# Scan levels: queries without zeros, and the level products head by head on row halves

## The chip, the core and the metric

One core of one Trainium2 chip runs the whole program. The metric is the device time of one execution in microseconds (us), the median of several runs. The engines named here are PE (TensorE: matrix products; its weight loads are listed apart, as PEld), DVE (VectorE), ACT (ScalarE), POOL (GpSimd) and SP (SyncE, which issues weight transfers). The program's buffers lie in SBUF; `ps` is PSUM, eight banks of 128 partitions by 512 fp32 values.

## The reference, cut to what matters

Two blocks of a network on 512 tokens of width 1024. The second block has two layers, and each of them has, among its token mixers, a gated linear recurrence (HGRN2) that runs forward and backward over the tokens:

```python
def _hgrn2_scan(q, k, v, logf):        # q, k, logf: 512 tokens x 6 heads x 64
    ...                                # bc = running sum of logf inside a chunk
    # o_t = sum over s <= t of  (q_t . k_s . exp(bc_t - bc_s)) v_s,  per head,
    # and a state that is carried from chunk to chunk

o_f = _hgrn2_scan(qr, heads(k_f), vr, heads(logf_f))
o_b = flip(_hgrn2_scan(flip(qr), flip(heads(k_b)), flip(vr), flip(heads(logf_b))))
o_r = o_f + o_b
```

The decay `exp(bc_t - bc_s)` is different for each of the 64 key channels of a head, so it has to be put into the queries and the keys before they are multiplied. It is everything in fp32.

## The kernel before

**Units.** The program treats the scan of one layer (it has two such scans, one at about 2058 to 2176 us of the profiled span, one at about 2862 to 2984 us) as six units: three blocks of 128 partitions, each with two heads of 64 key channels (head 0 in partitions 0 to 63, head 1 in 64 to 127), times two directions (d = 0 and 1; u = 2 b + d). Blocks are numbered `blk` over both scans.

**Pairs.** The 512 tokens are four tiles of 128. Products between different tiles, and the plain diagonal, are the pair products (L1246): 64 rows by 128 weight columns, 128 token columns, the two heads in turn on the two row halves of the array, each head into a bank of its own (`pair_bank`: banks 0 and 1 for even j - d, 2 and 3 for odd). ACT copies them out (L1910).

**Levels.** What is left inside a tile of 128 tokens is done in seven levels of halving, `LEVELS = [64, 32, 1, 2, 4, 8, 16]` (in this order; index li). On a level with half length m each block of 2m tokens has m queries and m keys on its two sides, decayed to the border between them. DVE writes the exponents of all seven levels of a unit into `WL` (L2619, L2620), ACT takes the exponential of all seven at once (L1887), DVE multiplies the key side by the keys (`weigh_levels`, L2642), POOL multiplies the query side by the queries (`queries`, L2962) and writes it into a buffer of its own, `level_queries(v)`, in spare columns of X and H (`resid` and `hbuf` in the profile). v counts the levels through both scans. Then PE multiplies: four products per level, one per tile t (L1264). The 128 weight columns are the tile's tokens with both heads' channels in the rows; the moving operand has 128 columns, of which the first 64 are the queries of head 0 with zeros in rows 64 to 127, the last 64 those of head 1 with zeros in rows 0 to 63. The zeros are written once per scan (L3001, L3002). One bank of 512 columns per level, in turn over banks 1, 2, 3, 0, 1, 2, 3 for li = 0 to 6.

**Taking.** ACT copies the levels li = 0 and 1 into the diagonal tiles of `AM` (L1928), in order and after all pairs of the unit; DVE merges li = 2 to 6 (`merge`, L2661, two predicated copies per level, one per head). `level_taken` counts both. A level's product waits for its query (`query_ready`), for the keys (`level_weighed`) and, from li = 4 on, for the bank: level v - 4 has been taken.

**Order of PE in a unit.** Pair products; a piece of the next layer stage's product that needs no scan result (`early`, L1311: ten 128x512 records per unit from the first levels on); for d = 0 and b >= 1 the sums of squares of the block before (`sum_rec`, L1330); the seven levels; for d = 0 the spread of its inverse root (`spread_rec`, L1339); for d = 1 the sum over the values (L1279), which waits until all 14 levels of the block have been taken. The first pair product of the next unit waits for all but the last two levels, those into banks 2 and 3 for all levels.

**Order of DVE in a unit.** `level_exponents(u+1)`, `weigh_ends(u+1)` (L2630, L2631), a finishing step of an earlier block (L2668, L2672, L2677), `merge(u)`, `weigh_levels(u+1)`. **ACT:** pair copies, a scaled copy for POOL (L1949), levels 0 and 1, `level_decays(u+1)` (L1887), a copy of sums, and the decays of the ends. **POOL:** `queries(u)`, an addition for the early piece (L2995), for every second unit the sum of the two directions' keys (L2983) and the power for the inverse root (L2973). POOL may run eight levels ahead of PE: `if v >= 8: pool.wait_ge(level_ready, v - 7)`.

All order is written out by hand, with semaphores; there is no planner.

Of the kernel before, what the change touches and what calls it, by code (L numbers as in the profile page):

```python
# [10 lines left out]
ALU = mybir.AluOpType  # L11
# [3 lines left out]
P = 128  # L15
D = 1024
KT = D // P
S = 512
C = 256
T = S + C  # L20
# [218 lines left out]
def build(nc, a, out):  # L239
    PHASES, CHUNKS = plan()  # L240
    with ExitStack() as ctx:
# [10 lines left out]
        X = sb("resid", [P, KT, T])  # L252
# [171 lines left out]
        def level_queries(v):  # L424

            k = v % 8
            return (X, H)[k // 4][:, 2 * (k % 4):2 * (k % 4) + 2, S:T]
# [486 lines left out]
        def level_bank(v):  # L914

            return (v % 7 + 1) % 4
# [64 lines left out]
        def _(pe):  # L981
# [234 lines left out]
            def scan(i):  # L1216
                n = scan_phases.index(i)
                for b in range(3):
                    blk = 3 * n + b
                    for d in range(2):  # L1220
# [5 lines left out]
                        for j in range(d, 4):  # L1226
                            if j == d and blk + d >= 1:

                                pe.wait_ge(level_taken, 14 * blk + 7 * d - 2)
# [22 lines left out]
                        for li in range(7):  # L1252
# [7 lines left out]
                            if li >= 4:  # L1260

                                pe.wait_ge(level_taken, v - 3)
                            for t in range(4):
                                mm = nc.tensor.matmul(ps[:, level_bank(v), t * P:(t + 1) * P], WL[:, 7 * (1 - d) + li, t * P:(t + 1) * P],  # L1264
                                                      level_queries(v)[:, t // 2, t % 2 * P:(t % 2 + 1) * P], start=True, stop=True)
# [223 lines left out]
        def _(act):  # L1489
# [359 lines left out]
            def scan(i):  # L1849
# [62 lines left out]
                def take_levels(u):  # L1912

                    blk, d = 3 * n + u // 2, u % 2
                    for li, m in enumerate(LEVELS[:PLAIN]):
# [7 lines left out]
                        for hx in range(2):  # L1923
                            for k in range(64 // m):
                                s0 = 2 * m * k + m * d
                                t0 = 2 * m * k + m * (1 - d)
                                from_ = ps[s0:s0 + m, level_bank(v), :].rearrange("p (t h x) -> p h t x", t=4, h=2)[:, hx, :, k * m:(k + 1) * m]
# [89 lines left out]
        def _(dve):  # L2017
# [577 lines left out]
            def scan(i):  # L2595
# [49 lines left out]
                def merge(blk, d):  # L2645

                    dve.wait_ge(pair_taken, pair_index(blk, d, 1, 3) + 1)
                    for li in range(PLAIN, 7):
# [9 lines left out]
                        for hx in range(2):  # L2658
                            dst = diagonal(hx).rearrange("p t (b x m) -> p t x b m", x=2, m=m)[:, :, 1 - d]
                            src = ps[:, level_bank(v), :].rearrange("p (t h b m) -> p h t b m", t=4, h=2, m=m)[:, hx]  # L2660
# [72 lines left out]
        def _(pool):  # L2733
# [173 lines left out]
            for i, ph in enumerate(PHASES):  # L2907
# [35 lines left out]
                elif kind == "scan":  # L2943
                    n = scan_phases.index(i)

                    def queries(u):
# [4 lines left out]
                        for li, m in enumerate(LEVELS):  # L2951
                            v = 42 * n + 7 * u + li
                            if v >= 8:

                                pool.wait_ge(level_ready, v - 7)
                            w = WL[:, 7 * (1 - d) + li, :].rearrange("p (t b x m) -> p t x b m", t=4, x=2, m=m)[:, :, 1 - d]
                            q = QR[:, b, :].rearrange("p (t b x m) -> p t x b m", t=4, x=2, m=m)[:, :, 1 - d]
                            dst = level_queries(v).rearrange("p a (c h b m) -> p a h c b m", c=2, h=2, m=m)
                            for hx in range(2):
                                rows = slice(64 * hx, 64 * hx + 64)  # L2960
                                for half in range(2):
                                    x = nc.gpsimd.tensor_tensor(dst[rows, half, hx], w[rows, 2 * half:2 * half + 2],  # L2962
                                                                q[rows, 2 * half:2 * half + 2], ALU.mult)
                            x.then_inc(query_ready, 1)
# [34 lines left out]
                    for half in (X, H):  # L2999
# [90 lines left out]
```

## Time and profile before

| | |
|---|---|
| median of 3 runs | 3423.84 us (3414.9 to 3428.85) |
| profiled execution | 3424.76 us |
| its span | 3422.7 us, so 2.06 us lie around the span |
| mean granted TensorE clock | 0.984 of full |
| PE busy | 3270.0 us |
| DVE, POOL, ACT busy | 2080.9, 1569.0, 968.0 us |

In the rows, PEclk is the granted clock of TensorE as a share of 2.4 GHz: 1.00 is the upper level, 0.50 the lower one (1.2 GHz). An fp32 product is two records, each with a weight load of its own: "x8" of L1264 is one level before the change. An idle time in brackets names what ended it.

### The profile page before, as it was taken

Reading aid. Unit: us, or ns where it says so; the run is one execution under the profiler, and the core shown is the slowest. Engines: PE = TensorE matmul, PEld = TensorE weight load, DVE = VectorE, ACT = ScalarE, POOL = GpSimd, SP = SyncE. Lnnn points to the kernel's source line nnn. Section 1 sums busy time; section 2 is a strip of 40 time slices with the busy share of each in tenths; the row PEclk is TensorE's granted clock in tenths of the full one; section 3 lists DMA queues with packets and bytes.
Section 4 is the critical chain, followed back from the end, with each engine's and each line's share of the span. In section 5 each row is a group of like instructions: output and inputs, shape, how many; then the busy total and the mean of one; then the engine's idle time right before and its main releaser. Section 6 shows DMA issues by size and latency. Waiting matters only on the chain. (4 is left out here: it accounts for less than half of the span.)

```text
span 3422.7 us, 44858 instructions
## 1 busy us (share of the span) xinstructions
PE 3270.0 (96%) x16138; PEld 2504.5 (73%) x16138; DVE 2080.9 (61%) x3509; ACT 968.0 (28%) x2213; POOL 1569.0 (46%) x1534
## 2 busy tenths in 40 slices
PE   7989999999999999999999978999999988999998
PEld 5666555555556967888888945688888865688887
DVE  7567756544444387455555668488764776656554
ACT  2066211001021165211122256322212236432211
POOL 1054323222235424544454548465645547755554
PEclk9999999999999999999999999999999998999999
DMA  7300223333312110344432200244443210022222
GB/s 251 125 23 2 99 86 123 117 117 105 123 57 65 66 38 14 105 158 165 157 124 85 85 20 14 77 149 156 156 150 102 88 46 16 20 92 87 87 87 80
DMA packets 91131, 317.88 MB, mean 93 GB/s; under 512 B 10817, under 2 KB 13153, under 8 KB 90913
## 3 DMA queue, kind: packets, MB, share of 16 engines
q1 hardware_dynamic: 64224, 218.34, 19.7%
q10 hardware_dynamic: 24768, 90.19, 7.2%
q0 software_dynamic: 1920, 6.49, 0.7%
q8 instruction: 132, 2.16, 0.3%
q14 instruction: 87, 0.70, 0.1%
HBM read 312.88 MB, written 2.10 MB: 92 GB/s over the span
## 5 line engine op out<-in xcount | busy, mean ns | idle before, releaser
L1354 PE MATMUL ps<-arena 128*128 128x256 f32 (+1 forms) x3744 | 952.4, 408 | 0.2
L1354 PEld LDWEIGHTS ps<-arena 128*128 128x128 f32 x3744 | 710.8, 190 | 205.0 <-issue 1.7
L2792 POOL TENSOR_TENSOR arena<-ring,arena 128x512 f32<-128x512 f32 (+1 forms) x140 | 181.6, 1297 | 837.0 <-PE ps L1354 837.0
L1354 PE MATMUL ps<-arena,ring 128*128 128x256 f32 (+1 forms) x2032 | 525.1, 410 | 3.1 <-ACT arena L1708 3.1
L1354 PE MATMUL ps<-hbuf,ring 128*128 128x256 f32 (+1 forms) x1824 | 471.6, 409 | 5.0 <-ACT hbuf L1815 2.0
L1354 PEld LDWEIGHTS ps<-arena,ring 128*128 128x128 f32 x2032 | 385.3, 190 | 119.8 <-ACT arena L1708 6.3
L1354 PEld LDWEIGHTS ps<-hbuf,ring 128*128 128x128 f32 x1824 | 349.0, 193 | 113.3 <-ACT hbuf L1815 16.2
L2330 DVE TENSOR_TENSOR arena<-ps,arena 128x256 f32<-128x256 f32 (+1 forms) x192 | 86.0, 448 | 357.0 <-PE ps L1354 235.9
L2217 DVE CUSTOM_DVE_ANT_0 aring<-aring,csil,adab 128x1024 f32<-128x1024 f32 x176 | 261.8, 1508 | 1.7
L2335 DVE SCALAR_TENSOR_TENSOR resid<-ps,mod,resid 128x256 f32<-128x256 f32 (+2 forms) x296 | 137.4, 482 | 185.4 <-PE ps L1354 180.3
L2775 POOL TENSOR_TENSOR arena<-ring 128x512 f32<-128x512 f32 (+1 forms) x140 | 181.2, 1294 | 141.3 <-PE ps L1354 133.2
L2335 DVE SCALAR_TENSOR_TENSOR resid<-arena,mod,resid 128x256 f32<-128x256 f32 (+1 forms) x168 | 109.2, 669 | 210.9 <-ACT arena L1708 207.6
L1708 ACT ACTIVATE arena<-ps 128x256 f32<-128x256 f32 (+1 forms) x152 | 62.9, 414 | 609.9 <-PE ps L1354 580.7
L2786 POOL TENSOR_TENSOR arena<-ring 128x512 f32<-128x512 f32 (+1 forms) x140 | 219.0, 1564 | 13.6 <-PE ps L1354 13.6
L1699 ACT ACTIVATE arena<-ps 128x256 f32<-128x256 f32 (+1 forms) x168 | 68.0, 405 | 476.0 <-PE ps L1354 465.7
L2781 POOL TENSOR_TENSOR arena<-arena,ring 128x512 f32<-128x512 f32 (+1 forms) x140 | 193.3, 1380 | 20.5 <-PE ps L1354 2.5
L2862 POOL TENSOR_SCALAR arena<-arena,small 128x512 f32<-128x512 f32 (+2 forms) x144 | 97.8, 691 | 209.1 <-DVE small L2098 209.1
L1354 PE MATMUL ps<-hbuf,arena 128*128 128x256 f32 (+1 forms) x672 | 175.8, 404 | 0.0
L2792 POOL TENSOR_TENSOR csil<-ring,junk 128x512 f32<-128x512 f32 x40 | 52.0, 1301 | 223.4 <-PE ps L1354 164.6
L1354 PEld LDWEIGHTS ps<-hbuf,arena 128*128 128x128 f32 x672 | 127.7, 190 | 34.4
L1672 ACT ACTIVATE rstd<-ps 128x256 f32<-128x256 f32 (+1 forms) x180 | 73.5, 408 | 253.6 <-PE ps L1354 236.3
L2424 DVE SCALAR_TENSOR_TENSOR arena<-arena 128x512 f32<-128x512 f32 x88 | 140.9, 1601 | 3.1
(327 smaller groups left out, 5209.3 us busy)
## 6 DMA issues: line engine op xcount, KB each, us to landing
aring<-in_ada ACTq DMA_DIRECT2D x172, 512.0 KB, 4.7
ring<-in_mlp SPq DMA_DIRECT2D x128, 512.0 KB, 3.8
ring<-in_up SPq DMA_DIRECT2D x88, 512.0 KB, 3.3
ring<-in_in SPq DMA_DIRECT2D x56, 512.0 KB, 3.3
ring<-in_down SPq DMA_DIRECT2D x32, 512.0 KB, 3.6
ring<-in_odd_in SPq DMA_DIRECT2D x24, 512.0 KB, 3.2
arena<-in_ada SPq DMA_DIRECT2D x16, 512.0 KB, 13.8
ring<-in_out SPq DMA_DIRECT2D x16, 512.0 KB, 3.2
```

The costliest lines, as they stand in the source:

```text
L1354: return nc.tensor.matmul(ps[:, bank, 0:p.tw], w, x, start=start, stop=stop, skip_group_check=True)
L1672: nc.scalar.activation(P1B[:, 0:tw], ps[:, XB[n % 2], 0:tw], ACT.Copy).then_inc(quick_act, 1)
L1699: nc.scalar.activation(second_sum(i, n)[:, 0:tw], ps[:, XB[n % 2], 0:tw], ACT.Copy).then_inc(quick_act, 1)
L2217: nc.vector.tensor_tensor_reduce(wt, wt, csil[:, 0, :], 1.0, adab[:, layer, nb:nb + 1], ALU.mult, ALU.add, mod[:, layer, nb, 0:1]).then_in ...
L2330: return nc.vector.tensor_tensor(home(p, half, lo, lo + tw), turned_view(p, product), turned_view(p, kept), ALU.add)
L2335: x = nc.vector.scalar_tensor_tensor(out=X[:, blk, a_:b_], in0=src[:, a_ - lo:b_ - lo], scalar=mod[:, layer, p.gate + blk, s_:s_ + 1], in1 ...
L2424: nc.vector.scalar_tensor_tensor(out=v, in0=u[:, 2:S + 2], scalar=CFW[:, blk, 2:3], in1=v, op0=ALU.mult, op1=ALU.add).then_inc(conv_out, 1)
L2775: nc.gpsimd.tensor_tensor(s[0], f1[:, 0:h], f1[:, h:2 * h], ALU.add).then_inc(wsum_ready, 1)
L2781: nc.gpsimd.tensor_tensor(s[1], s[0], f0[:, 0:h], ALU.subtract).then_inc(wsum_ready, 1)
L2786: nc.gpsimd.tensor_tensor(s[2], f0[:, 0:h], f1[:, 0:h], ALU.subtract).then_inc(wsum_ready, 1)
L2792: nc.gpsimd.tensor_tensor(s[3], f0[:, h:2 * h], s[1], ALU.subtract).then_inc(wsum_ready, 1)
L2862: nc.gpsimd.tensor_scalar(v, v, small[:, 12 + i % 4:13 + i % 4], 1.0, ALU.mult, ALU.mult).then_inc(pair_scaled, 1)
```

## The change

- POOL's queries of a level become one instruction of 128 partitions by 256 values (four tiles by 64), in place of four of 64 by 128. The buffer of a level is half as large, so there are 16 of them instead of 8, and POOL may run 16 levels ahead. The zeros and the four memsets per scan go.
- PE multiplies a level head by head, in turn on the row halves: eight products per level (16 records), each with 64 rows, 128 weight columns and 64 moving columns. Head 0 goes into one bank, head 1 into the next, 256 columns of each.
- So a level takes two banks. The pairs of banks are (2, 3), (0, 1), (2, 3), ... for li = 0, 1, 2, ...; from li = 2 on a level waits until level v - 2 has been taken (`v - 1` in the count). The first pair product of a unit waits for one level more than before.
- ACT and DVE read the same values from the new places, with as many instructions of the same sizes.

```diff
         def level_queries(v):
-            k = v % 8
-            return (X, H)[k // 4][:, 2 * (k % 4):2 * (k % 4) + 2, S:T]
+            k = v % 16
+            return (X, H)[k // 8][:, k % 8, S:T]
-        def level_bank(v):
-            return (v % 7 + 1) % 4
+        def level_bank(v, hx):
+            return 2 * ((v % 7 + 1) % 2) + hx
...
-                                pe.wait_ge(level_taken, 14 * blk + 7 * d - 2)
+                                pe.wait_ge(level_taken, 14 * blk + 7 * d - 1)
...
-                            if li >= 4:
-                                pe.wait_ge(level_taken, v - 3)
+                            if li >= 2:
+                                pe.wait_ge(level_taken, v - 1)
                             for t in range(4):
-                                mm = nc.tensor.matmul(ps[:, level_bank(v), t * P:(t + 1) * P], WL[:, 7 * (1 - d) + li, t * P:(t + 1) * P],
-                                                      level_queries(v)[:, t // 2, t % 2 * P:(t % 2 + 1) * P], start=True, stop=True)
+                                for hx in range(2):
+                                    rows = slice(64 * hx, 64 * hx + 64)
+                                    mm = nc.tensor.matmul(ps[:, level_bank(v, hx), 64 * t:64 * t + 64],
+                                                          WL[rows, 7 * (1 - d) + li, t * P:(t + 1) * P],
+                                                          level_queries(v)[rows, 64 * t:64 * t + 64], start=True, stop=True)
...
-                                from_ = ps[s0:s0 + m, level_bank(v), :].rearrange("p (t h x) -> p h t x", t=4, h=2)[:, hx, :, k * m:(k + 1) * m]
+                                from_ = ps[s0:s0 + m, level_bank(v, hx), 0:256].rearrange("p (t x) -> p t x", t=4)[:, :, k * m:(k + 1) * m]
...
-                            src = ps[:, level_bank(v), :].rearrange("p (t h b m) -> p h t b m", t=4, h=2, m=m)[:, hx]
+                            src = ps[:, level_bank(v, hx), 0:256].rearrange("p (t b m) -> p t b m", t=4, m=m)
...
-                            if v >= 8:
-                                pool.wait_ge(level_ready, v - 7)
+                            if v >= 16:
+                                pool.wait_ge(level_ready, v - 15)
...
-                            dst = level_queries(v).rearrange("p a (c h b m) -> p a h c b m", c=2, h=2, m=m)
-                            for hx in range(2):
-                                rows = slice(64 * hx, 64 * hx + 64)
-                                for half in range(2):
-                                    x = nc.gpsimd.tensor_tensor(dst[rows, half, hx], w[rows, 2 * half:2 * half + 2],
-                                                                q[rows, 2 * half:2 * half + 2], ALU.mult)
-                            x.then_inc(query_ready, 1)
+                            dst = level_queries(v).rearrange("p (t b m) -> p t b m", t=4, m=m)
+                            nc.gpsimd.tensor_tensor(dst, w, q, ALU.mult).then_inc(query_ready, 1)
...
-                    for half in (X, H):
-                        spare = half[:, :, S:T].rearrange("p k (c h v) -> p k h c v", c=2, h=2)
-                        nc.gpsimd.memset(spare[0:64, :, 1], 0.0)
-                        nc.gpsimd.memset(spare[64:P, :, 0], 0.0).then_inc(pool_step, 1)
-                        steps[0] += 1
-                        pool.wait_ge(pool_step, steps[0])
```

## Rows read from the trace of the kernel before

**Rows 1.** The page, part 1: busy time, share of the span, instructions.

```profile
PE 3270.0 (96%) x16138; PEld 2504.5 (73%) x16138; DVE 2080.9 (61%) x3509; ACT 968.0 (28%) x2213; POOL 1569.0 (46%) x1534
```

**Rows 2.** Line L1264: idle time before it, what ended it (us, times).

```profile
  POOL resid L2962: 14.8, 20
  POOL hbuf L2962: 14.1, 13
```

**Rows 3.** First scan by unit: busy us of PE, PEld, DVE, ACT, POOL; PEclk.

```profile
2057.89:2075.88 17.99, 13.97 (x98) 12.30 (x97) 11.76 (x29) 11.81 (x27) 15.98 (x32) 0.81 0.06 20
2095.96:2112.58 16.62, 15.77 (x133) 12.44 (x131) 12.06 (x28) 10.49 (x22) 15.60 (x28) 1.00 0.04 12
2112.58:2135.16 22.58, 18.55 (x107) 11.39 (x107) 22.00 (x48) 12.75 (x32) 21.22 (x39) 0.92 0.03 10
```

**Rows 4.** Groups by shape, POOL: busy us, mean ns, idle before.

```profile
L2962 POOL TENSOR_TENSOR resid<-arena 64x128 f32<-64x128 f32 x176 | 88.0, 519 | 8.5 <-issue 2.7
L2837 POOL TENSOR_TENSOR arena<-arena 128x256 f32<-128x256 f32 x24 | 15.9, 676 | 0.0
```

**Rows 5.** Timeline of PE, first scan: start us, us.

```profile
2051.30 6.66 PE L1311 MATMUL ps<-hbuf,ring 128*128 128x512 f32 x10 [4.71 <-ACT junk L1949]
...
2057.89 1.83 PE L1246 MATMUL ps<-arena 64*128 64x128 f32 x28
...
2062.30 3.80 PE L1264 MATMUL ps<-resid,arena 128*128 128x128 f32 x16 [0.82 <-POOL resid L2962]
2067.08 1.16 PE L1264 MATMUL ps<-resid,arena 128*128 128x128 f32 x8 [0.98 <-POOL resid L2962]
...
2103.93 0.95 PE L1330 MATMUL ps<-heads,arena 128*128 128x2 f32 x8
...
2129.88 5.35 PE L1279 MATMUL ps<-arena 128*64 128x512 f32 x16 [2.07 <-DVE arena L2661]
...
2138.74 4.56 PE L1311 MATMUL ps<-hbuf,ring 128*128 128x512 f32 x10
...
2143.94 3.82 PE L1264 MATMUL ps<-hbuf,arena 128*128 128x128 f32 x32
...
2166.95 3.65 PE L1279 MATMUL ps<-arena 128*64 128x512 f32 x16 [0.85 <-DVE arena L2661]
```

**Rows 6.** Timeline of DVE, first scan.

```profile
2056.81 2.44 DVE L2642 TENSOR_TENSOR arena<-arena 128x256 f32<-128x256 f32 x7 [7.25 <-ACT arena L1887]
...
2068.33 1.32 DVE L2661 COPY_PREDICATED arena<-arena,ps 128x256 f32<-128x256 int32 x2 [2.71 <-PE ps L1264]
...
2075.99 0.76 DVE L2661 COPY_PREDICATED arena<-arena,ps 128x256 f32<-128x256 int32 x2 [1.12 <-PE ps L1264]
2076.65 4.12 DVE L2642 TENSOR_TENSOR arena<-arena 128x256 f32<-128x256 f32 x7
...
2147.24 5.35 DVE L2661 COPY_PREDICATED arena<-arena,ps 128x256 f32<-128x256 int32 x10 [2.88 <-ACT arena L1928]
```

**Rows 7.** Timeline of ACT, unit 4 of the first scan.

```profile
2146.01 1.10 ACT L1928 ACTIVATE arena<-ps 32x128 f32<-32x128 f32 x4 [0.25 <-PE ps L1264]
```

**Rows 8.** Groups by shape, weight loads of the first scan: busy, mean ns.

```profile
L1246 PEld LDWEIGHTS ps<-arena 64*128 64x128 f32 x192 | 12.0, 187 | 9.2 <-ACT arena L1910 4.0 <-issue 2.4 <-DVE arena L2661 2.1
...
L1339 PEld LDWEIGHTS ps<-ident,small 128*64 128x64 f32 x43 | 2.3, 136 | 1.6 <-POOL small L2973 1.4
```

**Rows 9.** Chosen stretches: length, busy PE, PEld, DVE, ACT, POOL; PEclk.

```profile
1000.50:1004.00 3.50, 3.50 (x33) 3.50 (x33) 1.03 (x4) 0.94 (x2) 2.44 (x5) 1.00 0.34 81
1004.50:1007.50 3.00, 2.59 (x8) 2.01 (x9) 1.20 (x3) 0.06 (x1) 2.86 (x3) 0.50 0.21 71
...
2127.80:2130.60 2.80, 0.73 (x5) 0.34 (x6) 2.60 (x7) 2.15 (x8) 2.58 (x5) 1.00 0.02 6
2130.80:2134.00 3.20, 3.20 (x10) 0.96 (x8) 3.20 (x7) 0.00 (x0) 3.07 (x6) 0.50 0.00 0
```

**Rows 10.** Timeline of PE around 1001 us: what runs before the clock falls.

```profile
1001.44 2.82 PE L1167 MATMUL ps<-ones,arena 128*128 128x1 f32 x24
```

## The prediction

> **What bounds the kernel now.** I read the page first: TensorE is busy 96% of the span [rows 1], so what doesn't shorten or delay TensorE's own sequence changes nothing. Then I asked for the line of the level products. All its waits for POOL come to 14.8 + 14.1 = 28.9 us over both scans [rows 2], and PEld's waits are in that number together with PE's, so what PE itself lost is about half of it. That is a cap on what faster queries can give directly. Then the windows by unit and the timelines, to see where the waits lie. In unit 0 POOL sets the pace: it is busy 15.98 of 17.99 us, and the levels run from 2062.30 (first product) to 2076.65 (last merge done) [rows 3, 5, 6]. In unit 2 PE is busy 15.77 of 16.62 us, in unit 3 DVE 22.00 of 22.58 us [rows 3]: there POOL has caught up, four levels run without a gap in 3.82 us [rows 5], and the last wait before the values' product is for DVE's merge ([2.07 <-DVE], [0.85 <-DVE], rows 5). So the queries bound one unit in six; the others are bound by PE's order and by DVE's merges.
>
> **Queries.** A level's query is now four POOL instructions of 519 ns in the mean, 2.1 us; the nearest row for the new one is a 128x256 sum of POOL, 676 ns [rows 4]. Seven levels take some 5 us instead of 15. POOL drops out of the chain: in unit 0 the first product can start at about 2062.1 and never waits for a query again. The memsets lie before the scan in time that POOL spends waiting for ACT; I cost them at nothing.
>
> **Level product.** Before, a level is 8 records at 0.11 us, 0.9 us (3.82 for four, less the tail of the last). Is that the columns that stream, or the weights? The two-column products of L1330 tell: 8 records in 0.95 us, the same pitch as with 128 columns, so a 128-column weight load takes all of that pitch [rows 5]. The pair products, 64 rows in turn on two halves, run 28 records in 1.83 us, 0.06 us each: two halves at once, each again at 0.11 us [rows 5]. The new level has 16 records of that kind, so 16 x 0.06 = 0.9 us: no change, since the weights set the pace and only the streamed columns are halved. Loads of 64x128 take 187 ns in the record, those of 128x64 only 136 [rows 8]: the time goes with columns, not rows. The Trainium skill says the same (TensorE: Matmul & The Clock Gate, section "LDWEIGHTS (loading the stationary operand)": time is columns over 1.2 GHz, whatever the number of rows); the trace agrees. Bounds: 0.45 us if a half-height load with 64 columns took half, 0.9 us as taken. I take 0.9.
>
> **Two buffers in place of four.** A level is complete 1.16 us after its first record (the x8 row), DVE's merges take 1.32 us each for levels 2 and 3 and 0.76 for levels 4 to 6, with 0.1 between them 5.35 in all [rows 5, 6]. With P the start of the first level, ACT's copies of levels 0 and 1 end at P + 3.2 (2143.94 to 2147.11 in unit 4) and DVE starts merging at P + 3.3, 2147.24 [rows 5 to 7]. Now level 4 starts when level 2 is merged, D + 1.35 with D the start of merging, complete at D + 2.5, in time; level 5 starts when level 3 is merged, D + 2.8, complete D + 3.95, where DVE is ready at D + 3.65: 0.3 us late; level 6 follows at D + 3.7, complete D + 4.85. The merges end at D + 5.7 instead of D + 5.35, and DVE hears of the last level by a semaphore more: +0.4 us in each of 10 units (all but the two units 0), **+4 us**. Next in line, PE's values or pairs, waits for exactly this.
>
> **The clock.** This is the term that decides. Where the granted clock fell, PE had either stood idle much or streamed little. 1000.5 to 1004.0: PE and PEld busy for 3.50 of 3.50 us, but with one-column products (24 records of L1167); the next stretch is at 0.50 [rows 9, 10]. So weight loads by themselves don't hold it up. 2127.8 to 2130.6, the tail of a unit's levels and the wait for the merge: 0.73 us of PE, then 0.50, and the values' product took 5.35 us in place of 3.65 [rows 5, 9]. After the change a level streams half the columns in the same time, and from level 2 on its products come with gaps of 0.3 to 0.5 us. I expect the clock to fall in the second half of nearly every unit's levels, and to stay low until the values' product (odd units) or the early piece (even units) has run for a while. The prices, from rows at either level:
> - In unit 0 the clock is already low at the start: two levels took 3.80 us [rows 5]. Full-height products brought it back; half the columns won't. Seven levels at 1.75 us from 2062.1 end at 2074.4, the last merge at about 2075.3, against 2076.65. POOL's whole gain there is 1.4 us, in two scans **-3 us**.
> - In the other 10 units the last two levels run at 1.75 instead of 0.9: +1.7, less a little where DVE is late anyway: 1.6 x 10 = **+16 us**.
> - The values' product after levels: 5.35 instead of 3.65, for the 4 of 6 that now run at full clock, +1.7 each and +0.3 for the pairs that follow: **+8 us**.
> - After even units the spread, the pairs and the early piece: the ten-record piece took 6.66 us where it ran partly at the lower clock, against 4.56 [rows 5], +2.1 x 6 = 12.6. After units 0 and 2 DVE ends last anyway, by some 1.3 and 1 us, in two scans -4.6; one of these stretches is already low before the change, -1: **+7 us**.
>
> **DVE beside a lighter POOL.** The seven multiplications of `weigh_levels` take 2.44 us with POOL idle and 4.12 with POOL at work [rows 6]: the two disturb each other. POOL's bursts are now shorter but still begin shortly before these (they wait for the same ACT exponential), so I take half: 0.9 us, and it only counts where DVE ends last, twice per scan, and there mostly under the lower clock: **-1 us** (bounds 0 and -7). The Trainium skill has this as shared SBUF interfaces (GPSIMD Engine Reference, section "Key points"); the trace agrees with 2.44 against 4.12 us.
>
> **Sum.** -3 + 4 + 16 + 8 + 7 - 1 = +31 us on the profiled 3424.76 us, 3456 us. That execution lies 0.9 us over the median of the runs, so against 3423.84 it is +0.9%. I call within 0.5% (17 us) no change; the runs of before spread over 14 us.
>
> **Rivals.**
> 1. *The clock holds.* For it: PE and PEld stay as busy by the record, and the gaps are under half a microsecond each. Against it: the one-column row [rows 9, 10]. Then unit 0 runs its levels at about the present clock pattern and ends some 3.3 us (scan 1) and 4.6 us (scan 2) earlier, DVE's shorter multiplications give 1.3 x 2 + 0.4 x 2, the two buffers cost 4: -7.9 - 3.4 + 4 = -7, 3417 us. No change that can be told. It decides if the granted clock in units 1 to 5 stays above 0.95. Chance 0.19.
> 2. *Row halves really double the rate*: 0.45 us per level. Against it: L1330's pitch. It takes 0.7 us off the way to ACT's takes in the three units bound by PE, 0.7 x 6 = 4.2, and the 4 us of the two buffers vanish: -7 - 8 = -15, 3409 us with the clock held, the only way to come near -0.5%. The Trainium skill speaks for this one (TensorEngine Tiling (Array Packing), section "Theoretical Speedup": up to 2x for a small dimension of 64); by it this rival would be the result. Together with further savings on DVE over -0.5%: chance 0.03; otherwise with the clock fallen it only softens the forecast.
> 3. *The clock stays low through whole units*, from the levels over pairs and early piece into the next levels: then also the first levels (+1.7) and more of the pairs and the early piece (+2) run slow in the 10 units, +37 more, 3490 us. Chance 0.08.
>
> **How the numbers follow.** The forecast and its neighbours (the clock falls in most units, sum +17 to +55) have 0.70. Slower by over 0.5%: 0.70 + 0.08 - a tail of 0.04 where it falls but costs less than 17 us = 0.74; within 0.5%: 0.19 + 0.04 = 0.23; faster 0.03. The range reaches down to 3417 for rival 1 only in part: I set 3422 to 3488, which leaves about 0.16 below and 0.04 above; the forecast's own range is 3442 to 3475.
>
> **What would show it.** L2962 as 84 instructions of some 0.7 us and no PE wait for POOL in the scans (queries). L1264 with 16 records in 0.9 to 1.1 us where the clock is 1.00 (product). Merges of a unit in 5.7 us, PE waiting for DVE inside the levels (two buffers). PEclk by unit at 0.6 to 0.85 from unit 0 to 5, where it is 0.81 to 1.00 now [rows 3], and L1279 at over 5 us in most of six places (clock). What would make it wrong: a granted clock that doesn't fall at half the streamed columns; or falls that begin only after the unit's last level, so that the 16 us are not paid.

## The result, and the profile after

The changed kernel takes 3455.76 us (median of 4 runs, 3453.76 to 3459.49), the kernel before 3423.28 (4 runs beside it): ratio 1.0098, interval 1.0076 to 1.0121. It is slower by about 1%, and the forecast was 3456. The profiled execution took 3453.76 us (span 3451.9), 29.0 more than that of before; the medians lie 32.5 apart.

Part 1 of the page of the changed kernel, against [rows 1]:

```profile
PE 3311.1 (96%) x16810; PEld 2531.1 (73%) x16810; DVE 2074.7 (60%) x3509; ACT 968.3 (28%) x2213; POOL 1458.5 (42%) x1274
```

PE's busy time rose by 41 us although it streams fewer columns; POOL has 260 instructions fewer. POOL's queries by shape, after, against [rows 4]:

```profile
L2962 POOL TENSOR_TENSOR resid<-arena 128x256 f32<-128x256 f32 x44 | 34.7, 821 | 15.0 <-issue 9.5 <-ACT arena L1890 5.5
L2962 POOL TENSOR_TENSOR hbuf<-arena 128x256 f32<-128x256 f32 x40 | 31.3, 814 | 15.2 <-issue 12.5 <-ACT arena L1890 2.5
```

84 instructions, 66.0 us in all; a level's query costs 0.82 us where it cost 2.1. The waits of PE alone for its level products in the first scan, after (us, times, longest); [rows 2] has both scans and the weight loads too:

```profile
PE ps L1266 <- DVE arena L2664: 4.2, 12, 0.7
...
PE ps L1266 <- ACT arena L1931: 1.2, 5, 0.2
...
PE ps L1266 <- POOL resid L2962: 0.2, 1, 0.2
```

So the change did what it says: PE waits for POOL once, for 0.2 us, where it had waited eight times, 6.9 us, in this scan. It now waits for DVE, twelve times, inside the levels. The timeline of PE in the first scan, after (start us, us; in brackets the idle time before and who ended it), against [rows 5] (the lines have moved: L1266 is a level, L1282 the values' product, L1342 the spread, L1314 the early piece):

```profile
2062.13 3.04 PE L1266 MATMUL ps<-resid,arena 64*128 64x64 f32 x48 [0.63 <-ACT arena L1913]
...
2080.06 1.11 PE L1266 MATMUL ps<-resid,arena 64*128 64x64 f32 x16
2081.00 2.12 PE L1266 MATMUL ps<-hbuf,arena 64*128 64x64 f32 x32
2083.36 1.11 PE L1266 MATMUL ps<-hbuf,arena 64*128 64x64 f32 x16 [0.24 <-ACT arena L1931]
2084.82 1.11 PE L1266 MATMUL ps<-hbuf,arena 64*128 64x64 f32 x16 [0.34 <-DVE arena L2664]
2086.24 3.61 PE L1266 MATMUL ps<-hbuf,arena 64*128 64x64 f32 x32 [0.31 <-DVE arena L2664]
2090.71 6.55 PE L1282 MATMUL ps<-arena 128*64 128x512 f32 x16 [0.86 <-DVE arena L2664]
...
2112.21 2.40 PE L1266 MATMUL ps<-resid,arena 64*128 64x64 f32 x32 [0.31 <-DVE arena L2664]
2114.54 1.97 PE L1342 MATMUL ps<-ident,small 128*64 128x128 f32 x16
2116.44 2.98 PE L1246 MATMUL ps<-arena 64*128 64x128 f32 x24
2119.35 5.10 PE L1314 MATMUL ps<-hbuf,ring 128*128 128x512 f32 x10
```

Three levels (48 records) take 3.04 us, one level 1.11 with its tail: about 1 us, as before. A unit's last two levels take 3.61 us in unit 1 and 2.40 in unit 2 (2.0 at the upper clock), then the values' product 6.55 instead of 3.65, or the spread 1.97 instead of 1.09. Windows of the changed kernel (length, busy us of PE, PEld, DVE, ACT, POOL, then PEclk, the granted clock): the six units of the first scan (units 1, 3 and 5 without their values' product), and behind them four stretches, from the fourth level of unit 1 to the first pair products of unit 2.

```profile
2057.91:2072.64 14.73, 11.98 (x157) 10.76 (x156) 12.72 (x32) 12.15 (x29) 11.61 (x14) 0.89 0.08 24
2072.64:2090.71 18.07, 16.31 (x143) 12.56 (x143) 15.15 (x34) 10.60 (x24) 8.29 (x10) 0.78 0.06 19
2097.19:2114.54 17.35, 15.85 (x172) 12.44 (x171) 7.53 (x16) 11.17 (x24) 4.93 (x5) 0.97 0.05 13
2114.54:2134.95 20.41, 18.67 (x164) 14.59 (x163) 16.32 (x37) 12.18 (x31) 10.28 (x13) 0.75 0.03 11
2141.50:2158.78 17.28, 15.78 (x172) 12.38 (x171) 7.50 (x16) 9.91 (x20) 4.85 (x5) 0.98 0.05 13
2158.78:2176.62 17.84, 16.09 (x163) 12.20 (x163) 10.35 (x20) 4.39 (x13) 4.96 (x6) 0.88 0.04 12
...
2083.40:2086.20 2.80, 2.18 (x32) 1.93 (x32) 2.59 (x5) 2.80 (x1) 0.64 (x1) 1.00 0.03 6
2086.40:2090.00 3.60, 3.45 (x32) 3.26 (x31) 1.44 (x5) 3.40 (x12) 3.43 (x5) 0.50 0.00 0
2090.80:2096.80 6.00, 6.00 (x16) 1.63 (x16) 6.00 (x17) 0.00 (x0) 1.03 (x2) 0.52 0.00 0
2097.19:2100.70 3.51, 2.90 (x42) 2.46 (x40) 3.19 (x7) 2.82 (x7) 0.00 (x0) 1.00 0.02 5
```

The clock falls after the fifth level, with PE busy 2.18 of 2.80 us on half the columns; it stays at 0.50 while two levels keep PE busy for 3.45 of 3.60 us, and at 0.52 through 6.00 us of the values' product; behind that it is at 1.00. In the second scan the levels of unit 0, the pairs behind them and half of the early piece ran at 0.50, 17.00 us in one stretch (2881.7 to 2898.7), with PE busy for 16.68 of them. In the records of PE one can add up where the time of both scans went, from the first start of each stage to the first start of the next:

| stage, both scans (us) | before | after | after, 128 columns (e1_wide) | before, two buffers (e5_lock) |
|---|---|---|---|---|
| levels of unit 0 | 27.0 | 20.7 | 19.4 | 27.0 |
| levels of units 2 and 4 | 25.8 | 34.9 | 32.8 | 32.5 |
| levels of units 1, 3, 5 | 55.6 | 61.5 | 62.3 | 62.6 |
| values' product (6) | 25.5 | 37.5 | 21.5 | 21.5 |
| spread, rest of the pairs, early piece after even units | 49.0 | 55.2 | 43.9 | 42.7 |
| all else | 57.6 | 57.7 | 57.7 | 57.4 |
| sum | 240.5 | 267.5 | 237.7 | 243.8 |

27.0 of the 29.0 us lie in the two scans. The other 2 can't be told from chance: what lies outside the scans is the same program in all twelve profiles, and takes 3177 to 3188 us in them. The last two columns are experiments, below.

### The profile page after: what moved, and what is told of

It reads as the page before. It is cut to its first block and busy times, and to the rows that moved or that the text cites. A ratio compares the mean times of both kernels' runs of the same rounds, so it can differ in the third digit from the quotient of the medians.

```text
span 3451.9 us, 45966 instructions
## 1 busy us (share of the span) xinstructions
PE 3311.1 (96%) x16810; PEld 2531.1 (73%) x16810; DVE 2074.7 (60%) x3509; ACT 968.3 (28%) x2213; POOL 1458.5 (42%) x1274
## 5 line engine op out<-in xcount | busy, mean ns | idle before, releaser
L2789 POOL TENSOR_TENSOR arena<-ring 128x512 f32<-128x512 f32 (+1 forms) x140 | 218.9, 1563 | 11.9 <-PE ps L1357 11.9
L2784 POOL TENSOR_TENSOR arena<-arena,ring 128x512 f32<-128x512 f32 (+1 forms) x140 | 193.4, 1382 | 20.4 <-PE ps L1357 2.3
## 6 DMA issues: line engine op xcount, KB each, us to landing
arena<-in_ada SPq DMA_DIRECT2D x16, 512.0 KB, 13.7
```

Source lines behind the costliest of these rows:

```text
L2784: nc.gpsimd.tensor_tensor(s[1], s[0], f0[:, 0:h], ALU.subtract).then_inc(wsum_ready, 1)
L2789: nc.gpsimd.tensor_tensor(s[2], f0[:, 0:h], f1[:, 0:h], ALU.subtract).then_inc(wsum_ready, 1)
```

## The experiments

The time of the two scans in the profiled execution is given beside the whole time, since the scans are 7% of it and a few us of them vanish in the spread of the runs. Each scan time comes from one profiled execution, so a difference of one or two us between two of them isn't shown. The ratios are to runs of the kernel before on the same chip: median 3423.66 us for e1, e3, e4 and e5, 3425.97 for e6, e7, e9 and e10, 3426.14 for e11 and e12.

**e1_wide: the changed kernel with its 64 moving columns streamed twice.** The number of columns differs from the changed kernel, and with it the place of the results in their banks, from which ACT and DVE read as many values as before (that part is not shown).

```diff
-mm = nc.tensor.matmul(ps[:, level_bank(v, hx), 64 * t:64 * t + 64],
+mm = nc.tensor.matmul(ps[:, level_bank(v, hx), t * P:(t + 1) * P],
                       WL[rows, 7 * (1 - d) + li, t * P:(t + 1) * P],
-                      level_queries(v)[rows, 64 * t:64 * t + 64], start=True, stop=True)
+                      level_queries(v)[rows, 64 * t:64 * t + 64].unsqueeze(1).broadcast_to([64, 2, 64]), start=True, stop=True)
...
```

> The changed kernel, but each level product streams its 64 query columns twice, so 128 columns per weight load, and each head's products fill a whole bank; nothing else differs (queries, waits, two bank pairs, order), and all values that are used are the same. Clock theory: the weight loads set the pace, so a level still takes 0.9 us at the upper level, but the streamed columns keep the clock up: no fall inside the levels, the values' product back from 5.9 to 6.6 us to 3.65 in most of its six places, the two scans (240.5 us before, 267.5 after the change, from the first pair product to the first product behind them) take 230 to 236 us, the whole about 3416 us. Rival, two buffers or row halves: if the gaps for DVE or the alternation on halves cost the time, the scans stay at 260 us or more, the whole at 3450. Rival, product paced by columns: a level takes longer than 0.9 us.

Measured: 3420.9 us (12 runs; ratio to before 0.9989, interval 0.9980 to 0.9999), scans 237.7. Timeline of PE and windows (units 1 and 2) of e1_wide:

```profile
2079.56 1.16 PE L1266 MATMUL ps<-hbuf,arena 64*128 64x128 f32 x16 [1.27 <-DVE arena L2665]
2080.97 2.06 PE L1266 MATMUL ps<-hbuf,arena 64*128 64x128 f32 x32 [0.25 <-DVE arena L2665]
2083.89 3.65 PE L1283 MATMUL ps<-arena 128*64 128x512 f32 x16 [0.86 <-DVE arena L2665]
```

```profile
2072.60:2087.50 14.90, 12.33 (x133) 8.03 (x131) 13.99 (x28) 8.97 (x19) 8.33 (x9) 1.00 0.07 23
2087.50:2104.50 17.00, 15.65 (x172) 12.06 (x170) 10.85 (x26) 10.79 (x22) 4.55 (x5) 1.00 0.05 13
```

The same products with twice the columns take the same time each (1.16 against 1.11 us a level), the clock stays at 1.00 in these units, and the scans take 29.8 us less than in the changed kernel. That is the whole slowdown: with everything else of the change in place, it comes with the streamed columns, and the granted clock goes with it. What is left is a gain of 2.8 us and not the 7 I had for a clock that holds; 237.7 is above the 230 to 236 that I expected, 3420.9 above 3416.

**e5_lock: the kernel before, where PE waits for a level to be taken as if there were two level buffers.** Its four banks stay, and so does the first pair product's wait.

```diff
-                            if li >= 4:
+                            if li >= 2:
...
-                                pe.wait_ge(level_taken, v - 3)
+                                pe.wait_ge(level_taken, v - 1)
```

> The kernel before with only the wait of two buffers (from the third level on a level waits until the level two before it has been taken); it still has four banks. Two buffers by my sum: +0.4 us in 10 units, +4 us, scans 244 to 246 us, the whole 3427 us, as long as the clock stays as it is; products stream 128 columns, so short gaps should not bring it down much. If waiting itself made most of the loss, +20 us or more.

Measured: 3428.37 us (10 runs; 1.0013, 1.0003 to 1.0024), scans 243.8: 3.2 us more than before, where the forecast had 4. Its column of the table shows that this is a difference of large terms. The levels of ten units take 13.7 us longer, since PE is held back; of that 6.3 come back after the even units, where PE no longer has to wait behind the spread, and 4.0 in the values' product. PE and windows of e5_lock around unit 3, against [rows 5, 9]:

```profile
2128.90 1.13 PE L1264 MATMUL ps<-resid,arena 128*128 128x128 f32 x8 [1.74 <-DVE arena L2661]
2130.32 3.65 PE L1264 MATMUL ps<-resid,arena 128*128 128x128 f32 x16 [0.29 <-DVE arena L2661]
2134.82 3.65 PE L1279 MATMUL ps<-arena 128*64 128x512 f32 x16 [0.85 <-DVE arena L2661]
```

```profile
2130.00:2134.70 4.70, 3.68 (x17) 3.47 (x16) 2.40 (x8) 2.47 (x9) 4.35 (x8) 0.64 0.01 3
2134.90:2138.40 3.50, 3.50 (x16) 0.98 (x16) 3.50 (x7) 0.00 (x0) 3.37 (x6) 1.00 0.00 0
```

Before, the wait of 2.07 us came behind the last level. The clock was still at 1.00 until 2130.60, 0.7 us into the values' product, and at 0.50 from 2130.80 on, and this product paid (5.35 us) [rows 5, 9]. With the two-buffer wait the gap lies ahead of the last levels; the clock falls there too (two levels take 3.65 us), but it is back at 1.00 when the values' product starts, which runs in 3.65.

**e3_pool: the kernel before with the queries of the changed one**, products on all 128 rows with four banks. The zeros are left out, so its products mix the two heads; the buffers' places, POOL's wait and the memsets, which change as in the changed kernel, are not shown.

```diff
...
-                                                      level_queries(v)[:, t // 2, t % 2 * P:(t % 2 + 1) * P], start=True, stop=True)
+                                                      level_queries(v)[:, t % 2 * P:(t % 2 + 1) * P], start=True, stop=True)
...
-                            for hx in range(2):
-                                rows = slice(64 * hx, 64 * hx + 64)
-                                for half in range(2):
-                                    x = nc.gpsimd.tensor_tensor(dst[rows, half, hx], ...)
+                            nc.gpsimd.tensor_tensor(dst, w, q, ALU.mult).then_inc(query_ready, 1)
...
```

> The kernel before with POOL's part of the change alone: one instruction of 128x256 per level, 16 buffers, no memsets; PE multiplies as before, 128 rows and 128 columns, four bank buffers. Its products mix the two heads, since the zeros are gone: that is left out of the computation. All theories: this is what faster queries are worth with neither row halves, nor two buffers, nor fewer columns. By my terms the scans gain 7.9 us in the units 0 and about 3 us by DVE beside a lighter POOL: 229 to 233 us for both scans instead of 240.5, the whole about 3413 us. If POOL's gain had been there and been eaten by the rest of the change, it shows here; if POOL was never worth anything, 3423.

Measured: 3423.12 us (12 runs; 0.9997, 0.9988 to 1.0006), scans 242.6, 2.1 more than before and 10 over the most that I expected (233). The levels of unit 0 do take 17.7 us instead of 27.0. PE and windows of e3_pool at the end of unit 1:

```profile
2087.81 1.13 PE L1264 MATMUL ps<-hbuf,arena 128*128 128x128 f32 x8 [0.39 <-DVE arena L2661]
2091.74 5.23 PE L1279 MATMUL ps<-arena 128*64 128x512 f32 x16 [2.80 <-DVE arena L2661]
```

```profile
2088.95:2091.70 2.75, 0.00 (x0) 0.00 (x0) 2.44 (x8) 2.63 (x10) 2.75 (x5) 0.97 0.00 0
2091.80:2095.00 3.20, 3.20 (x8) 0.94 (x10) 3.20 (x6) 0.00 (x0) 1.99 (x3) 0.51 0.02 5
```

PE is done early, stands idle for 2.8 us until DVE has merged, and the values' product then runs at 0.51 for its first 3.2 us. It takes 5.2 to 5.4 us in all six places, 31.6 us in sum against 25.5. Of the 9.3 us that unit 0's levels gain, nothing is left: PE idles instead, and the clock is low behind the gap.

**e12_pool_lock: e3_pool with the wait of e5_lock.** It mixes the heads as e3_pool does.

```diff
-                            if li >= 4:
+                            if li >= 2:
...
-                                pe.wait_ge(level_taken, v - 3)
+                                pe.wait_ge(level_taken, v - 1)
```

> The kernel before with the fast queries and the wait of two buffers, 128 columns and full rows (its products mix the two heads, since the zeros are gone: that is left out of the computation). Against the variant with 64 columns streamed twice (237.7 us for both scans) only the row halves differ. If row halves cost nothing: 236 to 239 us. If each turn between half-height and full-height products costs some 0.1 to 0.2 us, as the spread pieces suggest (1.05 us from one to the next with halves, 0.87 without), 2 to 5 us less: 233 to 236. It also tells why fast queries alone gave nothing: if the values' product is back at 3.65 us here, the wait of two buffers kept the clock that they lost.

Measured: 3422.36 us (10 runs; 0.9992, 0.9982 to 1.0001), scans 236.6, the values' product at 3.65 us in all six units. So the two scans are 6 us shorter than in e3_pool with a wait more; the whole times (0.9992 and 0.9997) don't tell the two apart. The fast queries are worth 7.2 us where the wait stands (243.8 - 236.6). To e1_wide it is +1.1 (237.7 - 236.6): row halves, with their pairs of banks and the first pair product's longer wait. That lies in the range that I gave for row halves that cost nothing, and it is 3.0 us more in the units 0 and 1.9 less elsewhere, so no cost is shown by it.

**e4_cols and e7_cols_lock: the kernel before with 64 moving columns, with four buffers and with the two-buffer wait.** The rows stay whole, POOL stays slow. Head 1's products are left out, and ACT and DVE read head 0's for both (not shown); e7_cols_lock has the wait of e5_lock besides.

```diff
-mm = nc.tensor.matmul(ps[:, level_bank(v), t * P:(t + 1) * P], WL[:, 7 * (1 - d) + li, t * P:(t + 1) * P],
-                      level_queries(v)[:, t // 2, t % 2 * P:(t % 2 + 1) * P], start=True, stop=True)
+mm = nc.tensor.matmul(ps[:, level_bank(v), t * P:t * P + 64], WL[:, 7 * (1 - d) + li, t * P:(t + 1) * P],
+                      level_queries(v)[:, t // 2, t % 2 * P:t % 2 * P + 64], start=True, stop=True)
...
```

> The kernel before, but a level product streams only the first 64 of its 128 columns (head 0; head 1's level values are left out, both heads take head 0's). Full rows, four buffers, POOL as before with four instructions. Clock theory: the same weight loads, half the streamed columns, so the clock falls in the levels as in the changed kernel, although there are no row halves and no two buffers: PEclk of the scans 0.75 to 0.88, scans 250 to 262 us instead of 240.5, the whole 3433 to 3445 us. Rival, row halves or the two buffers: no change from 240.5 us and 3423.

> The kernel before with the 64 columns (head 0 alone; head 1's level values are left out) and the wait of two buffers, full rows, POOL as before. Alone the columns gave 252.4 us for both scans and the wait 243.7. Clock theory: the two together space thinly streaming products, the clock falls inside the levels and they wait for each other at the lower clock: 264 to 272 us, the same as the changed kernel with four POOL instructions, so that row halves cost nothing. If they only add (+11.9 + 3.2), 255.6 us, and then row halves would be the rest, 12 us or more.

Measured: e4_cols 3439.54 us (5 runs; 1.0043, 1.0027 to 1.0059), scans 252.4: +11.9, in the range, with PEclk 0.85 over each scan. So thin columns lower the clock with whole rows and four buffers too. e7_cols_lock 3451.99 us (4 runs; 1.0080, 1.0060 to 1.0099), scans 272.8, just over the 272 that I gave at most: +32.3 on before, and +29.1 on e5_lock, close to what the columns cost on row halves (29.8). So the wait costs 3.2 us with full columns and 20.4 with half (272.8 - 252.4), and the columns cost 11.9 without the wait and 29.1 with it: of the 32.3 us, 17.2 come only where the two stand together.

The granted clock sorts the twelve kernels by their columns alone. Over a whole scan it is 0.77 to 0.85 in the five that stream 64 columns, with whole rows (e4, e7) and on row halves (the changed kernel, e6, e11), and 0.93 to 0.99 in the seven that stream 128.

**e6_four_pool: the changed kernel with each query in four POOL instructions.**

```diff
-                            nc.gpsimd.tensor_tensor(dst, w, q, ALU.mult).then_inc(query_ready, 1)
+                            for hx in range(2):
+                                rows = slice(64 * hx, 64 * hx + 64)
+                                for half in range(2):
+                                    x = nc.gpsimd.tensor_tensor(dst[rows, 2 * half:2 * half + 2], ...)
+                            x.then_inc(query_ready, 1)
```

> The changed kernel with its queries written by four POOL instructions of 64x128 per level again; PE, the two buffers and the 64 columns stay. If the fast queries had kept some of their gain under the fallen clock (3 us by the prediction's unit 0), this is 3 to 8 us slower than the changed kernel's 267.5 us for both scans: 270 to 275, the whole 3458 to 3463 us. If slower queries space the levels so that other places lose or keep the clock, it can come out either side of 267.5.

Measured: 3463.36 us (4 runs; 1.0110, 1.0090 to 1.0130), scans 277.4, over the 275 that I gave at most. The fast queries are worth 9.9 us even under the fallen clock, 7.7 of it in unit 0 (28.4 against 20.7 us of levels). That is more than the 3 I had.

**e9_inter, e10_inter_before and e11_inter_thin: the early pieces spread between the levels.** Ten records of 512 columns (L1311) stand ahead of each unit's levels in one piece; here they are put in by twos between the levels, so that PE streams wide while it waits for DVE. Unit 0 has no such pieces. e9_inter does it to e1_wide, e10_inter_before to the kernel before, e11_inter_thin to the changed kernel. ACT's copy and POOL's addition of the piece, which move back, are not shown.

```diff
-                        early(i, EARLY_AT.get((2 * b + d, "levels"), ()))
+                        m = 2 + 2 * b + d
+                        if d == 1:
+                            early_part(i, m, range(0, 2), True, False)
...
+                            ks = ({1: 0, 2: 1, 3: 2, 4: 3, 6: 4} if d == 0 else {2: 2, 3: 3, 6: 4}).get(li)
+                            if ks is not None and m > 2:
+                                early_part(i, m, range(ks, ks + 1), ks == 0, ks == 4)
...
```

> The first variant (64 columns streamed twice), with the pieces of the next stage's product spread between the levels instead of ahead of them: for direction 0 one of five after the levels 1, 2, 3, 4 and 6, for direction 1 two ahead and one after the levels 2, 3 and 6; ACT's copy of the piece and POOL's addition move back accordingly. Theory: in the two-buffer version PE idles in the levels 2 to 3 us per unit, which the pieces fill, and DVE's 16.5 us per unit (merges, multiplications, exponents) becomes the bound instead of PE's 18.7 to 19.6: both scans 205 to 225 us instead of 237.7, the whole 3392 to 3408. Rival: DVE's own chain and the later copies on ACT hold the units at 18.5 or more, so 230 to 238 us and 3417.

> The kernel before with the same spreading of the pieces, nothing else: four POOL instructions per level, zeros, four bank buffers. If DVE becomes the bound, POOL's 15 us of queries and 3.9 us of other work per unit of 16.5 become the next one: 225 to 235 us for both scans, the whole 3405 to 3415, behind the variant with fast queries; so faster queries would be worth something only once PE and the clock no longer hide them. Rival: same as the variant with fast queries within 3 us.

> The changed kernel (64 columns, once) with the pieces of the next stage's product spread between the levels, as in the two variants before. Clock theory: what the levels lack in streamed columns the pieces between them give, so the clock holds from unit 1 on: the values' product at 3.65 us in at least four of six places, both scans 230 to 245 us instead of 267.5, the whole 3410 to 3425 us. Rival: the fall comes with half-height, 64-column products whatever stands between them: 255 us or more.

Measured: e9_inter 3412.87 us (7 runs; 0.9964, 0.9951 to 0.9977), scans 231.9: not the 205 to 225 that I expected but the rival's 230 to 238, without a run that shows which part of its chain holds it there. e10_inter_before 3411.65 us (8 runs; 0.9964, 0.9951 to 0.9977), scans 230.6, 10.0 less than before and in the range, but level with e9_inter, where I had put it behind. e11_inter_thin 3448.91 us (4 runs; 1.0058, 1.0036 to 1.0080), scans 264.2, where I had expected 230 to 245 and 3410 to 3425 in all, though the values' product did come back to 3.65 us in five of six places. The loss has moved into the levels. Unit 4 of the first scan, PE busy without a gap, first in e11_inter_thin, then the same 123 records in e9_inter:

```profile
2138.99:2161.90 22.91, 22.91 (x123) 14.84 (x122) 6.14 (x15) 5.78 (x10) 6.73 (x8) 0.50 0.01 1
```

```profile
2136.96:2149.40 12.44, 12.44 (x123) 8.12 (x122) 7.50 (x17) 5.78 (x10) 6.74 (x8) 1.00 0.01 3
```

They differ in the columns of the level products, 64 against 128, and in the clock, and take 22.91 and 12.44 us. That alone doesn't tell which brought which. But e9_inter has a stretch that begins low as well. In both kernels the clock fell about when the levels of such a unit began, behind pair products and sums of the same kind and length. Here is unit 4 of e11_inter_thin, just before the fall:

```profile
2132.20:2139.00 6.80, 6.19 (x62) 4.00 (x58) 5.17 (x13) 3.45 (x9) 0.00 (x0) 1.00 0.00 0
```

and here unit 2 of e9_inter, from its fall on:

```profile
2098.60:2101.90 3.30, 3.30 (x27) 2.74 (x24) 2.26 (x5) 1.34 (x5) 0.72 (x1) 0.50 0.00 0
2102.00:2112.00 10.00, 10.00 (x90) 5.96 (x88) 5.04 (x11) 6.83 (x14) 5.94 (x8) 1.00 0.01 2
```

With 128 columns the clock is back within 3.4 us, with 64 it stays at 0.50 for the 23.9 us from 2139.0 to 2162.9, all with PE busy. The units 2 and 4 of the second scan do the same in e11_inter_thin (low for 20.5 and 23.9 us). I had taken idle time for half of the cause; here there is none, and the low stretch is the longest of all. Thin columns don't always bring a fall, though: the levels of the units 1 and 2 of e11_inter_thin's first scan ran at the upper clock throughout. And whole rows of 128 columns don't always end one soon: in unit 0 of the kernel before, second scan, four levels took 7.31 us (2871.67) at 0.56 in the mean. What sets off a fall is not settled by these runs.

e10_inter_before beats both kernels of the study without anything of the change, by 0.4% against before, and is level with e9_inter (0.9964 both). Part of why it isn't behind e9_inter, which has the fast queries, is seen in the pitch of a level and a piece in turn, PE of e9_inter and of e10_inter_before in unit 4:

```profile
2138.94 1.13 PE L1320 MATMUL ps<-hbuf,ring 128*128 128x512 f32 x2
2140.00 1.16 PE L1268 MATMUL ps<-hbuf,arena 64*128 64x128 f32 x16
2141.09 1.12 PE L1320 MATMUL ps<-hbuf,ring 128*128 128x512 f32 x2
```

```profile
2136.22 1.02 PE L1316 MATMUL ps<-hbuf,ring 128*128 128x512 f32 x2
2137.08 1.05 PE L1266 MATMUL ps<-hbuf,arena 128*128 128x128 f32 x8
2137.97 1.02 PE L1316 MATMUL ps<-hbuf,ring 128*128 128x512 f32 x2
```

A level and a piece take 2.15 us (2141.09 - 2138.94) where the level is on row halves, 1.75 where it is whole (2137.97 - 2136.22). Both of its steps are longer by 0.2 us, that from the piece to the level too (1.06 against 0.86), though the piece itself is the same: each change between half and whole rows costs 0.2 us. The Trainium skill (TensorEngine Tiling (Array Packing), section "Key Properties") says that changing the tiling mode drains the engine; the trace fits that, at 0.2 us a turn.

## Why the prediction was right

**The result as four steps, in two orders.** From before over e5_lock, e12_pool_lock and e1_wide to the changed kernel, in scan time: two-buffer wait +3.2, fast queries -7.2, row halves +1.1, half the columns +29.8. From before over e5_lock, e7_cols_lock and e6_four_pool: +3.2, then columns +29.1, row halves with POOL's other layout +4.6, fast queries -9.9. Either chain must end at 27.0, since it starts and ends at the same two kernels, and the first step is the same run in both; so the sums prove nothing. What counts is that three of the steps were measured in two surroundings, and that the columns are the large one in both. Without the two-buffer wait they cost 11.9 (e4_cols). The mechanism named as the deciding term, the clock that falls with half the streamed columns and gaps between the levels, is shown by this.

**By the terms of the sum:**

- *Queries.* Right in kind ([rows 2] gone, unit 0 no longer paced by POOL), the size off. Unit 0 gives back 6.3 us and not 3: 4.2 in the first scan, where it didn't start low as before ([rows 5]: two levels in 3.80 us; after, at 2062.13, three in 3.04), and 2.1 in the second, where the levels ran nearly as forecast, at 0.50 from about 2881.7 to their end. There the kernel before didn't start low either: its first two levels ran at 1.00.
- *Level product.* 0.9 us a level as taken, 3.04 us for three. Rival 2, the doubled rate, is out: 64 or 128 columns, 64 or 128 rows, it is 0.9 us or a little over. The Trainium skill's "up to 2x" (TensorEngine Tiling (Array Packing), "Theoretical Speedup") is seen for one product (0.06 us a record on row halves, 0.11 on whole rows), but the level has twice as many of them and gains nothing; it doesn't lead to this rival, as I had read it.
- *Two buffers.* +4 forecast, +3.2 by e5_lock; near, though made of +13.7 and -10.3, of which I saw neither, and it holds for full columns alone: with half of them the same wait costs 20.4 (e7_cols_lock against e4_cols). The forecast had the gaps as a reason for the fall, but gave them no price of their own.
- *Last two levels at the lower clock, +16.* The mis-sized term. With the two-buffer wait already there (e1_wide), half the columns add 1.3 us to the levels of all ten units (96.4 - 95.1) and 1.3 to those of the units 0. The last two levels do take longer, but not everywhere: 2.3 to 3.0 us in the even units, where the clock fell at their end, 2.3 to 3.7 in the odd ones, where DVE ends last in any case. I had discounted "a little" for that; it was nearly all. Against before, the levels of the ten units grew by 15.0 us, where the forecast had 16 here and 4 for the buffers; but 13.7 of them are there with full columns already (e5_lock).
- *Values' product, +8.* It is +12.0 against before, and +16.0 against e1_wide: 5.85 to 6.62 us in all six places, not 5.35, because the clock was low when it began or fell at once, and it has no wait in which the loss could hide.
- *After even units, +7.* +6.2 against before, but +11.3 against e1_wide: spread 1.97 for 1.09, the pairs up to 3.0 for 2.0, the early piece up to 6.06 for 4.56.
- *DVE beside a lighter POOL, -1.* The weighing multiplications went from 4.0 to 4.6 us to 2.5 to 4.2 in the changed kernel, but in e1_wide, where the clock is mostly at 1.00, five of ten still take 4.4 to 4.5: the one at 2105.31 meets POOL's queries of 2105.07 to 2108.52. So a part of this relief is owed to the shifted times. Its share was not measured by itself.

So +31 came within 2 us of the profiled 29.0 by luck as to size, since errors cancel: the price of the clock, 38 by my own terms (from -7 with the clock held to +31), was 29.8, and the kernel with the clock held gained 2.8 and not 7. The clock cost less in the levels, where it fell, than in the wide products behind them, which have no slack (27.3 of the 29.8).

**The rivals.** The clock holds (0.19): out, 0.75 to 0.89 in units 0, 1, 3 and 5 of the first scan. But units 2 and 4 are at 0.97 and 0.98, above the 0.95 named there, and only two of the six windows lie in the 0.6 to 0.85 that were to show the forecast; the test was too coarse, since the mean of a unit that ends at the fall doesn't hold its price. The clock stays low through whole units (0.08): in the changed kernel only in unit 0 of the second scan, where it lasts from the levels over the pairs into the early piece (17.0 us); elsewhere it is back in the 512-column work. e11_inter_thin has it in three units. (By its own terms this rival is 3493 us, not 3490.)

**Left open.** Four level buffers with row halves were not tried, nor a number of columns between 64 and 128. What sets off a fall is not known: pair products and sums of the same length ended in one in some units and not in others. Why e3_pool, with PE idle for 2.75 us, and e12_pool_lock, with 2.38, end on different sides is told by the place of the gap (behind the last level or ahead of three), but no run moved the gap alone. And of the 14 us that the profiled execution of e10_inter_before gains, 4 lie outside the scans, within what this part varies by itself.

## What to carry to other kernels

In these kernels the products that streamed wide also kept TensorE's clock up, so taking out half the streamed columns where the weights set the pace saved nothing and slowed the products behind: compare the granted clock before looking at busy time. As far as e3_pool, e5_lock and e12_pool_lock tell, put an idle gap of TensorE ahead of full-size products that have slack and not ahead of the long one that hasn't, or fill it by cutting up wide work that stands nearby in one piece. And a shorter instruction on a helper engine is worth only what the next engine in line can take: here 7 to 10 us came out of 28.9 us of waits, and nothing at all where they ended in an idle TensorE.

## What the runs showed of the hardware that I had not expected

- A PE busy for 22.91 of 22.91 us at a granted clock of 0.50, beside 12.44 us for the same 123 records at 1.00, with twice the columns in the level products. The Trainium skill (TensorE: Matmul & The Clock Gate, section "What's actually happening") has the clock set by "how busy the PE has been recently"; by the busy time of the profile the trace does not agree.
- A wait more can shorten a stage: 242.6 to 236.6 us for both scans from e3_pool to e12_pool_lock, by a clock that is up when the values' product runs (3.65 instead of 5.2 to 5.4 us). The whole times don't show it.
- 0.2 us for each turn between products on row halves and on whole rows, in PE's pitch.
